# PEER in one run of tiles: query, up and down tiles behind one another, with key scores and the choice of sixteen begun between the query tiles

## The reference, cut to what matters

```python
def peer(h, w_q, sub_keys, u, v):
    T, D = h.shape
    q = (h @ w_q).reshape(T, PEER_HEADS, 2, PEER_QDIM // 2)
    ...
    sv, si = lax.top_k(s, PEER_TOPK)
    cand = (sv[:, :, 0, :, None] + sv[:, :, 1, None, :]).reshape(T, PEER_HEADS, PEER_TOPK * PEER_TOPK)
    fv, fi = lax.top_k(cand, PEER_TOPK)
    i1 = jnp.take_along_axis(si[:, :, 0], fi // PEER_TOPK, axis=-1)
    i2 = jnp.take_along_axis(si[:, :, 1], fi % PEER_TOPK, axis=-1)
    idx = (i1 * PEER_NKEYS + i2).reshape(T, PEER_HEADS * PEER_TOPK)
    g = jax.nn.softmax(fv, axis=-1).reshape(T, PEER_HEADS * PEER_TOPK).astype(h.dtype)
```

## Time and profile before

| | |
|---|---|
| median of 3 runs | 4343.5 us (4341.31 to 4346.03) |
| the profiled execution | 4343.25 us, of which 4341.5 us are the span |
| TensorE products busy | 4151.9 us (96%) |
| VectorE busy | 3027.0 us (70%) |
| ScalarE busy | 1807.5 us (42%) |
| GpSimd busy | 37.9 us (1%) |
| mean granted clock of TensorE | 0.984 of full speed |

### The profile page before, as it was taken

One profiled execution on the slowest core, in us unless ns is written; L12 is line 12 of the kernel. 1 busy time (PEld: TensorE's weight loads), 2 busy tenths in 40 slices (PEclk: granted clock), 3 DMA queues, 4 the chain that ended last, 5 costly groups with the idle time before them and its releaser, 6 DMA issues. The chain is left out here.

```text
span 4341.5 us, 81588 instructions
## 1 busy us (share of the span) xinstructions
PE 4151.9 (96%) x30549; PEld 3796.1 (87%) x30549; DVE 3027.0 (70%) x5239; ACT 1807.5 (42%) x2671; POOL 37.9 (1%) x54
## 2 busy tenths in 40 slices
PE   9999999999997899999999999999998899999998
PEld 8977999779894699899888898998886699899887
DVE  5566565555526469887888598878885569887887
ACT  4345343343324344444333444443333444444333
POOL 0000000000000001000000010000000000000000
PEclk9999999999999999999999999999999999999999
DMA  6644766346320157556776575557771267456775
GB/s 231 217 145 160 233 204 232 133 144 232 119 82 20 59 179 230 165 176 195 234 235 208 179 228 170 176 188 235 235 223 61 72 200 228 158 175 204 234 235 183
DMA packets 298266, 783.49 MB, mean 180 GB/s; under 512 B 32912, under 2 KB 132240, under 8 KB 297232
## 3 DMA queue, kind: packets, MB, share of 16 engines
q1 hardware_dynamic: 298000, 779.78, 56.2%
HBM read 728.27 MB, written 51.38 MB: 180 GB/s over the span
## 5 line engine op out<-in xcount | busy, mean ns | idle before, releaser
L262 ACT ACTIVATE ring_hi<-ring 128x1024 fp32r<-128x1024 f32 x1173 | 1243.3, 1061 | 1943.5 <-PE banks L283 1218.7
L268 DVE TENSOR_TENSOR ring_lo<-ring,ring_hi 128x1024 fp32r<-128x1024 f32 x1173 | 1436.1, 1225 | 716.0 <-ACT ring_hi L262 702.3
L279 PE MATMUL banks<-h_parts,ring_hi 128*128 128x256 f32 x4824 | 1208.5, 288 | 16.4 <-ACT ring_hi L262 15.1
L280 PE MATMUL banks<-h_parts,ring_hi 128*128 128x256 f32 x4824 | 1186.7, 284 | 0.0
L279 PEld LDWEIGHTS banks<-h_parts,ring_hi 128*128 128x128 f32 x4824 | 926.8, 192 | 32.0 <-issue 21.5
L280 PEld LDWEIGHTS banks<-h_parts,ring_hi 128*128 128x128 f32 x4824 | 928.0, 192 | 0.3
L294 PE MATMUL banks<-h_parts,ring_hi 128*128 128x512 f32 x3048 | 763.5, 392 | 0.7 <-DVE h_parts L1914 0.6
L283 PE MATMUL banks<-h_parts,ring_lo 128*128 128x256 f32 x4824 | 678.0, 283 | 0.9 <-DVE ring_lo L268 0.6
L294 PEld LDWEIGHTS banks<-h_parts,ring_hi 128*128 128x128 f32 x3048 | 548.1, 189 | 100.1 <-issue 2.0
L283 PEld LDWEIGHTS banks<-h_parts,ring_lo 128*128 128x128 f32 x4824 | 623.3, 192 | 2.5 <-DVE ring_lo L268 2.5
L297 PEld LDWEIGHTS banks<-h_parts,ring_lo 128*128 128x128 f32 x3048 | 415.8, 190 | 29.7
(11 more groups left out here) (239 smaller groups left out, 3813.7 us busy)
## 6 DMA issues: line engine op xcount, KB each, us to landing
ring<-peer_u_dram SPq DMA_DIRECT2D x384, 512.0 KB, 4.1
ring<-peer_v_dram SPq DMA_DIRECT2D x384, 512.0 KB, 3.7
big<-mod_w_dram SPq DMA_DIRECT2D x96, 512.0 KB, 4.7
act_store<-acts_out SPq DMA_DIRECT2D x384, 128.0 KB, 3.2
scratch<-act_store SPq DMA_DIRECT2D x384, 128.0 KB, 3.5
ring<-ffn_gate_dram SPq DMA_DIRECT2D x88, 512.0 KB, 4.0
ring<-ffn_up_dram SPq DMA_DIRECT2D x88, 512.0 KB, 3.6
ring<-ffn_down_dram SPq DMA_DIRECT2D x88, 512.0 KB, 3.6
```

Of the source, the lines that this page charges most:

```text
L262: self.nc.scalar.activation(self.hi[:, n % 2], self.ring[:, self.slot(j)], ACT.Copy).then_inc(self.count("tile_hi").sem, 1)
L268: self.nc.vector.tensor_tensor(self.lo[:, self.slot(j)], self.ring[:, self.slot(j)], self.hi[:, n % 2].bitcast(F32), ALU.subtract).then_in ...
L279: self.nc.tensor.matmul(out, w, b_hi, start=opens and m == 0, stop=False)
L280: self.nc.tensor.matmul(out, w, b_lo, start=False, stop=False)
```

## The change

`peer` no longer calls `linear`. The 16 query tiles (Q = 16) become tiles 0 to 15 of the run of `experts`, the up tiles 16 to 143, the down tiles 144 to 271. One barrier per call goes. The hardware loop of the query part is written out.

- **TensorE**: `query(j)` puts tile j into bank j % 4. Behind each odd tile j = 2p + 3 it runs `score(p)`: the scores of head p, both halves and both token blocks, 4 products of 128x128 into bank 6 or 7. score(0) to score(6) stand behind query tiles 3 to 15, score(7) behind the second up tile. score(0) waits for the keys (`tables`).
- **ScalarE**: behind `split_hi` of tile j+2 it copies the product of tile j to `q`, and behind even tiles j = 2p + 4 it moves the scores of head p to `s`. The last two moves stand behind gelus.
- **VectorE**: `sixteen` takes a list of rows. The 32 rows are worked in 4 batches of 8 rows (2 heads), each with its four passes. Before a batch asks for the scores of head p, `scores_of(p)` splits tiles until 2p + 7 are split, and then waits for the move. The wait for the last of the four passes stands only once behind all batches. `spend` may split up to tile Q + NS.
- **GpSimd**: the additions go by head, each behind the third pass of its batch.
- **SP**: fetches query tiles 4 to 15 and up tiles 0 to 3 in the same block; the keys are issued behind tile 5.

```diff
+            def score(p):
+                pe.wait_ge(taken.sem, taken.after(2 * p + 2))
+                pe.wait_ge(moved.sem, moved.after(p - 1))
+                if p == 0:
+                    pe.wait_ge(tables.sem, tables.after(16))
+                for t in range(NT):
+                    for m in range(2):
+                        last = nc.tensor.matmul(k.ps[:, 6 + p % 2, (2 * t + m) * P:(2 * t + m + 1) * P],
+                                                q[:, 2 * p + m, t * P:(t + 1) * P], keys[:, 2 * p + m], start=True, stop=True)
+                last.then_inc(scored.sem, 1)
...
-            for n, (t, g) in enumerate(groups):
-                pe.wait_ge(moved.sem, moved.after(n - 3))
-                for m in range(4):
-                    last = nc.tensor.matmul(k.ps[:, n % 4, m * P:(m + 1) * P], q[:, 4 * g + m, t * P:(t + 1) * P],
-                                            keys[:, 4 * g + m], start=True, stop=True)
-                last.then_inc(scored.sem, 1)
-            for e in range(NS):
-                rise(e)
+            for j in range(Q + NS):
+                if j < Q:
+                    query(j)
+                else:
+                    rise(j - Q)
+                p = (j - LAG + 1) // 2
+                if j % 2 and 0 <= p < HEADS:
+                    score(p)
...
-                if spent >= 1750 and tile < NS:
+                if spent >= 1750 and tile < Q + NS:
...
+            def scores_of(p):
+                nonlocal spent
+                while tile < 2 * p + LAG + 3:
+                    split()
+                    spent = 0
+                dve.wait_ge(moved.sem, moved.after(p + 1))
...
-            sixteen(NT * HP, s, left, sv, si, lambda n: dve.wait_ge(moved.sem, moved.after(n // 4 + 1)))
+            for b in range(HEADS // 2):
+                sixteen([t * HP + 4 * b + 2 * m + r for m in range(2) for t in range(NT) for r in range(2)], s, left, sv, si,
+                        lambda n: scores_of(n % HP // 2))
+            dve.wait_ge(top.sem, top.after(count))
...
+            for j in range(Q):
+                k.split_hi(act, j + 2)
+                act.wait_ge(done.sem, done.after(j + 1))
+                nc.scalar.activation(q[:, j], k.ps[:, j % R, 0:T], ACT.Copy).then_inc(taken.sem, 1)
+                move(j)
             for e in range(N):
-                k.split_hi(act, e + 2)
-                act.wait_ge(done.sem, done.after(e + 1))
+                k.split_hi(act, Q + e + 2)
+                act.wait_ge(done.sem, done.after(Q + e + 1))
                 act.wait_ge(k.act_stored[e % R].sem, k.act_stored[e % R].after(16 * (e // R)))
                 nc.scalar.activation(k.acts[:, e % R], k.ps[:, 4 + e % 2, 0:T], ACT.Gelu).then_inc(acted.sem, 1)
-                if e == exp_under:
+                move(Q + e)
+                if e == exp_under - Q:
...
-    linear(k, a.peer_q[layer], 2 * HEADS, 1, q, beside=[(keys, a.peer_k[layer])], ahead=first(a.peer_u[layer]))
```

More of the change, by code:

```diff
@@ L1707, in experts @@
     N, NS, STEPS = NKEYS, UNDER_SELECT, T // 4
-    u, v, h = a.peer_u[layer], a.peer_v[layer], k.parts[0]
+    Q, LAG = HP, 4
+    wq, u, v, h = a.peer_q[layer], a.peer_u[layer], a.peer_v[layer], k.parts[0]
+    taken, tables = k.count("product_taken"), k.dma("tables_loaded")
     G = k.region(0, NKEYS, T)
@@ L1729, in experts @@
     sides = sif.rearrange("p (n two) b -> p n two b", two=2)
-    groups = [(t, g) for t in range(NT) for g in range(HP // 4)]
+    by_block = s.rearrange("p (t r) n -> p t r n", t=NT)
     marks = k.scratch[:].rearrange("p (r side t n) -> p r side t n", r=2, side=2, t=B)
@@ L1745, in act_load @@
                 sp.dma_start(act_in[:, r], k.act_store[e]).then_inc(k.act_loaded[r].sem, 16)
+            for j in range(R, Q + R):
+                k.fetch(sp, j, 0, wq[j] if j < Q else u[j - Q])
+                if j == R + 1:
+                    sp.dma_start(keys, a.peer_k[layer]).then_inc(tables.sem, 16)
             for e in range(N):
                 j = e + R
-                k.fetch(sp, j, 0, u[j] if j < N else v[:, j - N])
+                k.fetch(sp, Q + j, 0, u[j] if j < N else v[:, j - N])
                 sp.wait_ge(acted.sem, acted.after(e + 1))
@@ L1760, in _ @@
                 for r in range(R):
-                    k.fetch(sp, N + R + r, i, v[:, i * R + (R + r)])
+                    k.fetch(sp, Q + N + R + r, i, v[:, i * R + (R + r)])
                     act_load(r, i, r + 1, i * R + (R + r))
@@ L1765, in _, with query @@
         def _(pe):
+            def query(j):
+                pe.wait_ge(taken.sem, taken.after(j + 1 - R))
+                k.three(pe, j, 0, [(k.ps[:, j % R, 0:T], c, h[:, 0, c], h[:, 1, c]) for c in range(KD)],
+                        True).then_inc(done.sem, 1)
+            def score(p):
[8 more added lines that the diff above has]
+                last.then_inc(scored.sem, 1)
             def rise(e):
                 pe.wait_ge(acted.sem, acted.after(e - 1))
-                k.three(pe, e, 0, [(k.ps[:, 4 + e % 2, 0:T], c, h[:, 0, c], h[:, 1, c]) for c in range(KD)],
+                k.three(pe, Q + e, 0, [(k.ps[:, 4 + e % 2, 0:T], c, h[:, 0, c], h[:, 1, c]) for c in range(KD)],
                         True).then_inc(done.sem, 1)
@@ L1783, in fall @@
                 pe.wait_ge(ready.sem, i * R + ready.after(r + 1))
[L1784 to L1793 removed]
+                k.two(pe, Q + N + r, i, falls, h[:, 0, r % 2], h[:, 0:2, r % 2]).then_inc(done.sem, 1)
+            for j in range(Q + NS):
[6 more added lines that the diff above has]
+                    score(p)
             for w in range(3):
@@ L1815, in _ @@
             pe.wait_ge(ready.sem, ready.after(N))
-            k.two_by_chunk(pe, 2 * N - 1, sorted(falls, key=lambda f: f[1]), h[:, 0, 1], h[:, 0:2, 1], summed)
+            k.two_by_chunk(pe, Q + 2 * N - 1, sorted(falls, key=lambda f: f[1]), h[:, 0, 1], h[:, 0:2, 1], summed)
             for c in range(2, KD):
@@ L1822, in _ @@
         def _(pool):
-            for n in range(NT * HEADS):
-                pool.wait_ge(top.sem, top.after(2 * NT * HP + 2 * n + 2))
+            for m in range(NT * HEADS):
+                p, t = m // NT, m % NT
+                n = t * HEADS + p
+                pool.wait_ge(top.sem, top.after(32 * (p // 2) + 16 + 4 * (p % 2) + 2 * t + 2))
                 nc.gpsimd.tensor_tensor(cand[:, n].rearrange("p (a b) -> p a b", b=16),
@@ L1852, in sixteen @@
                 nonlocal count
-                first, width = count, src.shape[2]
-                for n in range(rows):
+                first, width, many = count, src.shape[2], len(rows)
+                for n in rows:
                     arrive(n)
@@ L1857, in sixteen @@
                     spend(width)
-                for n in range(rows):
-                    dve.wait_ge(top.sem, top.after(first + n + 1))
+                for i, n in enumerate(rows):
+                    dve.wait_ge(top.sem, top.after(first + i + 1))
                     nc.vector.max_index(places[:, n, 0:8], values[:, n, 0:8], src[:, n])
@@ L1862, in sixteen @@
                     spend(2 * width + 300)
-                for n in range(rows):
-                    dve.wait_ge(top.sem, top.after(first + rows + n + 1))
+                for i, n in enumerate(rows):
+                    dve.wait_ge(top.sem, top.after(first + many + i + 1))
                     nc.vector.max(values[:, n, 8:16], rest[:, n]).then_inc(top.sem, 1)
                     spend(width)
-                for n in range(rows):
-                    dve.wait_ge(top.sem, top.after(first + 2 * rows + n + 1))
+                for i, n in enumerate(rows):
+                    dve.wait_ge(top.sem, top.after(first + 2 * many + i + 1))
                     nc.vector.max_index(places[:, n, 8:16], values[:, n, 8:16], rest[:, n]).then_inc(top.sem, 1)
                     spend(width + 75)
-                count += 4 * rows
-                dve.wait_ge(top.sem, top.after(count))
+                count += 4 * many
+            def scores_of(p):
[4 more added lines that the diff above has]
+                dve.wait_ge(moved.sem, moved.after(p + 1))
             def choose(w, base):
@@ L1922, in _ @@
             split()
-            sixteen(NT * HP, s, left, sv, si, lambda n: dve.wait_ge(moved.sem, moved.after(n // 4 + 1)))
+            for b in range(HEADS // 2):
+                sixteen([t * HP + 4 * b + 2 * m + r for m in range(2) for t in range(NT) for r in range(2)], s, left, sv, si,
+                        lambda n: scores_of(n % HP // 2))
+            dve.wait_ge(top.sem, top.after(count))
             nc.vector.tensor_copy(sif, si).then_inc(after.sem, 1)
-            sixteen(NT * HEADS, cand, cand_left, fv, fi, lambda n: dve.wait_ge(pairs.sem, pairs.after(n + 1)))
+            sixteen([t * HEADS + p for p in range(HEADS) for t in range(NT)], cand, cand_left, fv, fi,
+                    lambda n: dve.wait_ge(pairs.sem, pairs.after(NT * (n % HEADS) + n // HEADS + 1)))
```

(43 more changed lines are left out.)

## The result

The changed kernel takes 4313.1 us in the median of 4 runs (4308.44 to 4317.7); the kernel before, timed beside it, 4342.41 us. The ratio is 0.9933, 95% interval 0.992 to 0.9946: faster by 29.3 us, where 32 were forecast. The profiled execution took 4310.94 us, span 4309.1, 32.4 us less than the span before; it was the second fastest of the four.

The account below looks back on a forecast made before the run. TensorE bounds the kernel, except where it waits for VectorE's choice at the transposes. Per call 12.5 + 1.00 + 0.28 - 0.8 - 2.3 = 10.7 us, 32.1 for three: 4343.25 to 4311 us; own range 4309 to 4315, wide 4302 to 4324.

Parts of the forecast that it names:

- The wait at the transposes: Between up tiles and transposes, TensorE's wait for VectorE's choice goes wholly: -12.5 us a call.
- The low clock behind the wait: After TensorE's idle time at the transposes, the lower clock goes too: about 1.7 us, within the 12.5.
- The count: Tiles split when `choose` comes near: 52 before, 58 after, so the choice comes 10 tiles, 28.8 us, earlier.
- The margin of 14.5 us: At the transposes, VectorE would be ready 14.5 us early: 41.2 us from `choose` on against TensorE's 55.7.
- Boundary and table load: Gap between query tiles and scores goes, -1.00 us; table load at the first gelu is covered, -0.28 us a call.
- The choice's last operations: In `choose`, five more tiles go at VectorE's pace, 3.33 us against TensorE's 2.88: +2.3 us a call.
- The keys: Before the scores of head 0, TensorE waits for the keys' transfer: +0.8 us a call, 0.4 to 1.2.
- The written-out loop: In the query part, taken branches go, but tiles already stood 2.88 us apart: 0 us.
- A: Rival: waiting for keys and slower tiles in `choose` are hidden, 3.1 us a call unpaid: 4302 us, chance 0.14.
- B: Rival: VectorE's losses, such as beside GpSimd's additions, bring back a wait at the transposes: 4333 us, chance 0.12.
- C: Rival: choice work slows TensorE from tile 9 to 71, 26 us a call at 3.4 us distance: 4389 us, chance 0.05.
- D: Rival: no change, as the choice ends no earlier against the transposes: 4343 us, chance 0.03.

Follow-up runs that it names:

- the row of runs above: Changed kernel with scores and choice begun 4, 6, 8 or 12 tiles later: 4309.24, 4310.19, 4328.07 and 4350.29 us.
- The run twelve tiles later: Changed kernel with scores and choice begun twelve tiles later, tiles still joined: 4350.29 us, 1.0021 of the kernel before.
- keys first: Changed kernel with the keys as SP's first issue in the block, ahead of query tile 4: 4309.92 us, 0.9924 of the kernel before.
- the second edit: Changed kernel where two low parts may follow one operation of the choice; alone 4303.21 us, 0.9908 of the kernel before.
- the two edits together: Changed kernel with the keys issued first and two low parts allowed after one choice operation: 4300.2 us, 0.9906 of the kernel before.
- four tiles later: Changed kernel with scores and choice begun four query tiles later: 4309.24 us, 0.9924 of the kernel before.

## Why the prediction was right

*The wait at the transposes* was given 12.5 us a call. The low parts of tiles 59 and 60 are now 3.53, 3.52 and 3.52 us apart, where 16.09 stood: 12.56.

```profile
1752.10 1.12 PE L283 MATMUL banks<-h_parts,ring_lo 128*128 128x256 f32 x8
1753.06 0.82 PE L1823 MATMUL banks<-con,big 128*128 128x128 f32 x6
1755.63 1.12 PE L283 MATMUL banks<-h_parts,ring_lo 128*128 128x256 f32 x8
```

The low clock behind the wait shows in the table's third line, 1.9 to 2.3 us a call against 1.7. The count was one tile low on both sides (`choose` began with 53 split before and 59 after, not 52 and 58), so its difference of ten tiles held: VectorE took 41.2 us from `choose` on, TensorE 55.6, as forecast. The margin of 14.5 us came out as 14.4, and the row of runs above moves the choice across it and finds the wait where the count has it. This step is shown.

*Boundary and table load*, 1.0 and 0.28: there is no barrier. The third up tile, the one that waits for the first gelu, has its low part 3.76 us behind that of the second (1580.80 to 1584.56), which is a tile and a head's scores with nothing lost. The run twelve tiles later has both without keys' wait and without lateness. Its way to the first transposes is 1.22 us shorter than before; taking off the lateness of 0.66 that the kernel before had and adding the 0.83 us that its own first transpose waits, 1.39 are left for the two and for what the scores take less between the tiles, where 1.28 were forecast.

*The choice's last operations*, +2.3 us for lateness: 3.0 less 0.66 is 2.4, and removing all of it gained 3.0 us a call (keys first, with and without the second edit). Shown.

*The keys*, +0.8 us with 0.4 to 1.2 as bounds, were mis-sized for one call. The waits are 0.34, 3.12 and 0.29 us, and behind the long one the clock fell to 0.76 over four microseconds. The short ones cost 0.6 and 0.5 us (4.35 and 4.29 between two low parts where 3.77 were due). From the low part of tile 3 to that of tile 5 the second call takes 11.47 us instead of 6.65, so 4.8 us in place of 0.8:

```profile
2399.38 1.12 PE L283 MATMUL banks<-h_parts,ring_lo 128*128 128x256 f32 x8
2403.62 1.13 PE L1786 MATMUL banks<-big 128*128 128x128 f32 x8 [3.12 <-DMA big<-peer_k_dram]
2407.61 1.50 PE L283 MATMUL banks<-h_parts,ring_lo 128*128 128x256 f32 x8
2410.85 1.12 PE L283 MATMUL banks<-h_parts,ring_lo 128*128 128x256 f32 x8
```

```profile
2395.15 1.05 SPq L1752 DMA_DIRECT2D big<-peer_k_dram  x1
```

That accounts for the difference between its gain, 7.25, and the first call's, 11.16. I had bounded the wait by the landing times before, 5.6 to 6.4 us; now the issue of the second call took 1.05 us on SP, and the keys landed 8.3 us after its start. I had also ruled the clock out from one idle time of 0.84 us; that holds for the short waits only.

*The written-out loop* was given 0. Query tiles are 2.88 us apart in both kernels, so no stall shows. The Trainium skill ("Runtime: NRT & Kernel Launch", Instruction fetch mechanics) has the stall only for a taken branch whose target lies outside the fetched window; that the loop's target lay outside it, as the prediction took it, is not shown.

*The rivals.* A (additions hidden) is refuted for both additions; what it would have given is nearly what the two edits together give, 4300 us. B's mechanism is there: in each call three low parts take 1.49 to 1.69 us beside GpSimd's additions instead of 1.23. It costs nothing, since VectorE waits for high parts anyway; the margin is untouched. C did not come: before `choose` no distance is over 2.88 us but at the scores, the keys and, in the third call, the low clock of its first tiles, and small batches' waits on their own results have no price. D's condition, a choice that ends no earlier, came only with the choice twelve tiles later.

In sum, the first call gained 11.2 us for 10.7 forecast, the second 7.3 for the keys, and the third 10.1, its first query tiles having met a low clock (3.92 us between two low parts instead of 2.88). That is 28.5 us for 32.1. That the profiled span fell by 32.4, so close to the forecast, is luck: 3.9 us of it lie outside the calls' changed parts and fill the gap that the keys left. The mechanism and its main term hold without that luck.

## What to carry to other kernels

When one engine's long chain of work must be ready before another's next step, count its order in tiles of the other engine: the difference is a threshold, and only the part up to it is a gain. What begins earlier must not pull a transfer onto the critical chain; ask of every load when it is first read in the new order, and issue it first. Where a fixed rhythm mixes two kinds of work, compare its slowest stretch with the pace of the engine that waits: 3.33 against 2.88 us cost 3 us a call until the rhythm was allowed two low parts in one place.

## What I had not expected of the hardware

- An idle time of 1.48 us (and one of 0.19 or 0.64 just behind it) is followed by the full clock in one call and by 0.89 over 15 us in another of the same execution, and the stretches differ by 2.0 us. The start of a call is another such place. In the eleven traces with joined tiles, 25 calls have 1.54 us of idle time before their first query tile and tiles 2.88 us apart behind it; 8 calls have 1.85 us, and 3.50 to 3.92 us to the second low part. Which of the two comes first, the longer idle time or the low clock, is open. The changed kernel and the one with the keys first spread over 9 to 14 us, which hides an edit worth 5 us; how much of that spread such places make is not shown.
- The length of a wait does not settle the clock behind it. Waits for the keys of 2.1 to 2.6 us cost 0.2 us more than themselves (three calls), one of 3.1 us cost 1.7 more, and of three of 3.2 us two cost 1.8 more and one 0.2.
- The issue of the keys in the second call took 1.05 to 1.48 us on SP's queue in seven of the eight traces in which it stands behind tile 5 (0.56 in the eighth, four tiles later), and 0.43 in the other calls and, issued one tile later, in all three. Where TensorE waited for it, the wait was 2.1 to 3.1 us. Why this one issue is slow is open.
